# Seven-product input projection in the third and fourth block, and the second layer's modulation as float32 column tiles between the units of output projections

## The reference

```python
def modulation(cond, w, b):
    m = jax.nn.silu(cond) @ w + b          # (2 rows, 1024) @ (1024, 9216)
    return m.reshape(cond.shape[0], 1, N_MOD, D_MODEL)
def modulate_in(x, g_pre, mod, j):
    return rmsnorm(x, g_pre) * (1.0 + mod[:, :, 3 * j + 1]) + mod[:, :, 3 * j]
def gated_residual(x, out, g_post, mod, j, weight):
    return x + weight * mod[:, :, 3 * j + 2] * rmsnorm(out, g_post)
def swiglu(h, w13, w2):                    # w13: 1024 x 5632, w2: 2816 x 1024
    a, g = jnp.split(h @ w13, 2, axis=-1)
    return (jax.nn.silu(g) * a) @ w2
```

## Time and profile before

| what | value |
|---|---|
| runs | 2536.49, 2536.21, 2535.64 us; median 2536.21 us |
| profiled execution, its own time | 2541.83 us |
| its span | 2540.0 us, mean granted clock 0.995 |
| PE busy | 2476.5 us (97%), 15180 matmuls |
| DVE busy | 1581.6 us (62%) |
| ACT busy | 764.9 us (30%) |
| POOL busy | 224.6 us (9%) |
| bytes moved | 278.64 MB, mean 110 GB/s |

### The profile page before, as it was taken

How to read it: one execution, slowest core, us unless ns; L and a number is a source line. 1 busy time by engine, 2 the same in 40 slices (tenths; PEclk the granted TensorE clock), 3 DMA queues, 4 the chain that set the end, 5 groups by cost and what they waited for, 6 DMA issues and landing times. The chain is left out here.

```text
span 2540.0 us, 40285 instructions
## 1 busy us (share of the span) xinstructions
PE 2476.5 (97%) x15180; PEld 2295.7 (90%) x15180; DVE 1581.6 (62%) x2779; ACT 764.9 (30%) x1418; POOL 224.6 (9%) x299
## 2 busy tenths in 40 slices
PE   6999999999998899999999999999999999999998
PEld 5998999799888789989988998899799979989997
DVE  4887588734554678738875885233454458845864
ACT  4111111333444441111124211111331153523432
POOL 0000000201114210000002000000110011201211
PEclk9999999999999999999999999999999999999999
DMA  6554445333223335434551553222312223323332
GB/s 242 160 141 133 133 149 167 107 77 81 48 56 88 88 107 149 134 100 141 149 170 55 150 153 99 80 74 87 96 59 75 87 79 117 83 71 99 88 113 103
DMA packets 385035, 278.64 MB, mean 110 GB/s; under 512 B 39414, under 2 KB 354550, under 8 KB 383894
## 3 DMA queue, kind: packets, MB, share of 16 engines
q1 hardware_dynamic: 384918, 277.06, 36.4%
HBM read 270.04 MB, written 6.94 MB: 109 GB/s over the span
## 5 line engine op out<-in xcount | busy, mean ns | idle before, releaser
L1879 DVE TENSOR_TENSOR w_lo<-w_raw,w_hi 128x1024 fp32r<-128x1024 f32 (+1 forms) x363 | 354.5, 979 | 501.2 <-ACT w_hi L1303 496.8
L1303 ACT ACTIVATE w_hi<-w_raw 128x1024 fp32r<-128x1024 f32 (+1 forms) x363 | 309.2, 854 | 832.4 <-PE psum L921 425.3
L921 PE MATMUL psum<-hT_hi,w_hi 128*128 128x320 f32 x2432 | 554.8, 309 | 4.0 <-DVE w_lo L1879 3.3
L921 PE MATMUL psum<-hT_lo,w_hi 128*128 128x320 f32 x2432 | 554.1, 309 | 0.0
L921 PE MATMUL psum<-hT_hi,w_lo 128*128 128x320 f32 x2432 | 553.8, 309 | 0.0
L921 PEld LDWEIGHTS psum<-hT_hi,w_hi 128*128 128x128 f32 x2432 | 406.3, 188 | 5.7 <-DVE w_lo L1879 2.8
L921 PEld LDWEIGHTS psum<-hT_lo,w_hi 128*128 128x128 f32 x2432 | 406.8, 188 | 0.0
L921 PEld LDWEIGHTS psum<-hT_hi,w_lo 128*128 128x128 f32 x2432 | 406.6, 188 | 0.0
L1848 DVE SCALAR_TENSOR_TENSOR mod_acc<-ada_raw,cond_silu,mod_acc 128x256 f32<-128x256 f32 x896 | 365.4, 479 | 0.0
L848 PE MATMUL psum<-w_hi,act_hi 128*128 128x512 f32 x800 | 318.1, 398 | 4.6 <-DVE w_lo L1879 4.5
L849 PE MATMUL psum<-w_lo,act_hi 128*128 128x512 f32 x800 | 316.3, 395 | 0.0
(11 more groups left out here) (281 smaller groups left out, 3548.1 us busy)
## 6 DMA issues: line engine op xcount, KB each, us to landing
w_raw<-in_ffn_w_dram SPq DMA_DIRECT2D x156, 512.0 KB, 4.1
ada_raw<-in_ada_w_dram SPq DMA_DIRECT2D x128, 512.0 KB, 3.6
w_raw<-in_ffn_w_dram SPq DMA_DIRECT2D x148, 256.0 KB, 2.7
w_raw<-in_ab_w_in_dram SPq DMA_DIRECT2D x28, 512.0 KB, 4.1
w_raw<-in_sc_w_in_dram SPq DMA_DIRECT2D x24, 512.0 KB, 4.0
w_raw_next<-in_ffn_w_dram SPq DMA_DIRECT2D x20, 512.0 KB, 5.2
ada_first<-in_ada_w_dram SPq DMA_DIRECT2D x4, 2048.0 KB, 19.0
held_raw<-in_ffn_w_dram SPq DMA_DIRECT2D x28, 256.0 KB, 3.7
```

The lines of the kernel that those rows point to most:

```text
L921: last = mm(IN[p][0:width, h, 0:HT], a, b[:, k, h * HT:(h + 1) * HT], start=(k == 0 and a is hi and b is hT_hi), stop=(k == KD - 1 and a i ...
L1303: A(dst, src, ACT.Copy).then_inc(w_hi_ok, 1)
L1879: V.tensor_tensor(d_, a, b.bitcast(F32), ALU.subtract).then_inc(w_lo_ok, 1)
```

## The change

Three things are changed together.

1. `PLAIN` names s = 2 and s = 3 as well: 38 more pairs in seven-product form. These blocks also keep x in DRAM and load it again, and load gate, post-norm weights and the next block's column modulation (`load_gate`, `load_cols`) behind the last product of half 1, ahead of the third output unit's weights.
2. The jobs of s = 2 and s = 3 go. The nine modulations of layer 2 (`MODS`: three and one in s = 2, three and one in s = 3, one in s = 5) are made by TensorE in 8 steps each, 72 in all. A step is a float32 matmul on four column tiles: weights `csil[:, :, k]` (128x2), moving `ada_tile` (four times 256 columns), all four tiles into the first 256 columns of one PSUM bank. Steps stand behind output units (`STEP_AT`): in half 0 with three modulations 24 steps behind 17 of the units 1 to 17, with one modulation 8 steps behind 5 units, in half 1 one step behind each of the units 2 to 9. The tiles are 512 KB, in a ring of three, loaded by SP (`load_mods`); the first load of a phase stands behind the fifth output unit's weights (the fifth in half 0, the fourth in half 1) and behind four bias transfers. DVE adds the bias (`modulation_rows`, four operations a modulation) and SP stores the four pieces.
3. Banks, buffer slots and semaphore counts are generalised for these blocks (`out_bank`, `banks`, `RAW_SLOT`); the first output unit of such a half now waits for the last cross sum of the products.

```diff
@@ tables @@
-PLAIN = {5: (3, 0)}
+PLAIN = {2: (3, 0), 3: (3, 0), 5: (3, 0)}
...
-JOBS = {0: (0, 2 * D, (HF, HF), (3, 3)), 2: (1, 0, (HF, HF), (1, 1)), 3: (1, 6 * D, (HF, 0), (1, 0))}
+JOBS = {0: (0, 2 * D, (HF, HF), (3, 3))}
+MODS = {2: ([(1, 0), (1, D), (1, 2 * D)], [(1, 3 * D)]), 3: ([(1, 4 * D), (1, 5 * D), (1, 6 * D)], [(1, 7 * D)]), 5: ([(1, 8 * D)], [])}
+MW = 256
+STEP_AT = lambda half, n: [1 + j * 17 // 24 for j in range(8 * n)] if not half else [2 + j for j in range(8 * n)]
@@ SP: loads of the modulation tiles, called from load_out behind unit u's weights @@
+            def load_mods(ph, u):
+                n = len(ph["mods"])
+                at_u = STEP_AT(ph["half"], n)
+                for j in range(8 * n):
+                    if max(2, at_u[j] + 3 - 2 * ph["half"]) != u:
+                        continue
+                    g = 8 * ph["mb"] + j
+                    if j == 0:
+                        load_bias_rows(ph, 0)
+                        sp.wait_ge(prod_lo_ok, SEVEN * ph["g1"])
+                    if j >= 3:
+                        sp.wait_ge(mod_mm, MM(g - 3))
...
+                    dma(ada_tile[ph["half"]][slot][:], src).then_inc(ada_landed[slot], 16)
@@ PE: the steps, called behind every output unit @@
+            def modulation(ph, u):
+                n = len(ph["mods"])
+                bank = 0 if ph["half"] else 1
+                for j, at_u in enumerate(STEP_AT(ph["half"], n)):
+                    if at_u != u:
+                        continue
+                    g, k = 8 * ph["mb"] + j, j % 8
+                    if j == 0:
+                        pe.wait_ge(q_summed, U_CROSS(ph["g1"] - 1))
+                    elif k == 0:
+                        pe.wait_ge(mrow_ok, MROW(ph["mb"] + j // 8 - 1))
+                    slot, count = TILE(g)
+                    pe.wait_ge(ada_landed[slot], count)
+                    for i in range(4):
+                        last = mm(PS[32 * i:32 * i + 2, bank, 0:MW], csil[:, :, k], ada_tile[ph["half"]][slot][:, i, :], start=(k == 0), stop=(k == 7))
+                    last.then_inc(mod_mm, 1)
@@ PE: bank_free @@
-                            if t == 2:
+                            if t == NT - 1:
                                 pe.wait_ge(q_gated, G_ONE(ph["g1"] - 1))
-                                pe.wait_ge(q_summed, U_TWO(ph["g1"] - 1))
-                            if t == NT - 1:
-                                pe.wait_ge(q_summed, U_CROSS(ph["g1"] - 1))
...
+                        if seven(ph):
+                            if t == 0:
+                                pe.wait_ge(q_summed, U_CROSS(ph["g1"] - 1))
+                            if t >= 2:
+                                pe.wait_ge(out_evac, ph["oe"] + t - 1)
@@ DVE @@
+            def modulation_rows(ph, z):
+                b = ph["mb"] + z
+                dve.wait_ge(mod_mm, MM(8 * b + 7))
...
+                for i in range(4):
+                    rows = slice(32 * i, 32 * i + 2)
+                    V.tensor_tensor(mod_rows[ph["half"]][rows, :], PS[rows, 0 if ph["half"] else 1, 0:MW], mod_bias[rows, :], ALU.add).then_inc(mrow_ok, 1)
```

More of the change, by code:

```diff
@@ L266, in build @@
         assert tail + 8192 + 4096 + HT * 4 <= end, end - tail
+        mod_bias = at("mod_bias", [P, MW], end // 32 * 32 - MW * 4)
+        assert held_at + 3 * 4096 <= end // 32 * 32 - MW * 4
+        mod_rows = [at("mod_rows0", [P, MW], end // 32 * 32 - 2 * MW * 4), at("mod_rows1", [P, MW], held_at - MW * 4)]
+        assert tail + 8192 + 4096 + HT * 4 <= end // 32 * 32 - 2 * MW * 4
+        ada_tile = [[at(f"ada_tile{h}{z}", [P, 4, MW], (tail if h == 0 else j0) + z * 4 * MW * 4) for z in range(3)] for h in range(2)]
+        assert 3 * 4 * MW * 4 <= 8192 + 4096 and j0 + 3 * 4 * MW * 4 <= held_at - MW * 4
         more_hi = at("w_hi_more", [P, 3, KH, P], where["gate"], F32R)
@@ L638, in load_in, with late_rows @@
                         load_job(ph, -1, i)
+            def late_rows(ph):
+                n = len(ph["mods"])
+                last = len(out_units(ph)) - 1
+                for z in range(n):
+                    if STEP_AT(ph["half"], n)[8 * z + 7] + 7 > last:
+                        store_mod_rows(ph, z)
+                        assert z == n - 1
             def load_pairs(s, w, ph, c0):
@@ L860, in turn_x @@
                             pe.wait_ge(mrow_ok, plan[s - 1][-1]["bt"] + 1)
+                    if t == 1 and plan[s - 1][-1].get("mods"):
+                        pe.wait_ge(mrow_ok, MROW(plan[s - 1][-1]["mods_end"] - 1))
                     if t in (1, 4):
@@ L940, in pair_products @@
                         pe.wait_ge(out_evac, ph["oe"] - NT + (1 if q else 0))
+                    elif new == 0 and q == 2 and ph["mb"]:
+                        pe.wait_ge(mrow_ok, MROW(ph["mb"] - 1))
                     elif new == 1 and q == 0:
@@ L1027, in out_phase @@
                             bank_free(d, t)
-                        last = weights(d, k, OUT[d][t], t, k == 0, k == K - 1)
+                        last = weights(d, k, out_bank(ph, d, t), t, k == 0, k == K - 1)
                         if k == K - 1 and t < NT - 1:
@@ L1031, in out_phase @@
                     last.then_inc(pe_unit, 1)
+                    if seven(ph):
+                        modulation(ph, u)
                 if not held:
@@ L1050, in out_phase @@
                             turn_x(s + 1, t - 2)
-                        last = weights(1, k, OUT[1][t], t, z == 0, z == K - 1)
+                        last = weights(1, k, out_bank(ph, 1, t), t, z == 0, z == K - 1)
                         if t == NT - 1 and k in ring:
@@ L2021, in boundary @@
                 split_h(s, NT - 1)
+            def modulation_rows(ph, z):
+                b = ph["mb"] + z
+                dve.wait_ge(mod_mm, MM(8 * b + 7))
+                dve.wait_ge(bias_in, BIAS(b))
+                dve.wait_ge(mod_stored, STORED(b - 1))
+                for i in range(4):
+                    rows = slice(32 * i, 32 * i + 2)
+                    V.tensor_tensor(mod_rows[ph["half"]][rows, :], PS[rows, 0 if ph["half"] else 1, 0:MW], mod_bias[rows, :], ALU.add).then_inc(mrow_ok, 1)
             def out_phase(s, ph):
@@ L2034, in out_phase @@
                             split_held(s, ph, i)
+                    if seven(ph):
+                        for z in range(len(ph["mods"])):
+                            if min(STEP_AT(ph["half"], len(ph["mods"]))[8 * z + 7] + 4, len(units) - 1) == u:
+                                modulation_rows(ph, z)
                     z, r = divmod(u - 1 - LATE[ph["half"]] if late else u, 3)
-                    sooner = 2 if late and not final else 0
+                    sooner = 2 if (late or seven(ph)) and not final else 0
                     if sooner and u == K + 1:
```

104 lines of the change are left out of this document (75 added, 29 removed).

## The result

| | before | with the change |
|---|---|---|
| median of five runs | 2536.28 us | 2548.31 us |
| lowest to highest | 2535.64 to 2537.79 | 2546.09 to 2551.79 |
| profiled execution, its span | 2541.83 us, 2540.0 us | 2547.93 us, 2546.1 us |
| PE busy | 2476.5 us | 2467.1 us |
| matmul records | 15180 | 15288 |

The ratio is 1.0043, 95% interval 1.003 to 1.0055: slower by 12 us. The forecast was "the same" at 2539.2 us, range 2523 to 2557, with 0.38 for slower. The range holds the time, but by the 0.2% that I had set for no change the kernel is slower, and none of the rivals is the reason in the form in which I wrote it: of the one on column tiles and the clock (0.08) the clock did fall, but behind waits and for 9 us, where its price of 93 us was for tiles one after another.

A forecast was written before the change was run, and what follows sets the result against it. PE, busy 97% of the span, was taken as the bound. -58.75 (products) + 31.0 (steps) + 19.3 (visits) + 10.2 (first tiles) + 1.2 = +2.95 us on 2536.21 gave 2539.2 us, range 2523 to 2557.

The forecast's parts named there:

- the one on column tiles and the clock: Slower rival, output phases: column tiles of one bank run serially, or the clock falls; +93 us, 2632 us, chance 0.08.
- The products: Third and fourth blocks: seven-product input phases save 63.35 us; after later waits and sums of jobs, -58.75 us net.
- The steps: Output phases: 72 added modulation steps on PE at 0.43 us each, +31.0 us.
- The visit: Output phases: 55 changes from full width to column tiles and back, 0.35 us each, +19.3 us; lower end 4.4.
- The row of the attention: Profile row with half-width matmuls between full ones, source of the 0.35 us taken for each visit.
- The rival of cheap visits: Faster rival, output phases: a visit costs 0.08 us instead of 0.35; -14.9 us, 2524.3 us, chance 0.14.
- The first tiles: Half 0 of three blocks: PE waits for the first two tiles, 3.4 us a block, +10.2 us.
- late transfers: Slower rival, half 1: tiles land late behind consecutive units, 3 to 13 us each half; +16 us, 2555.2 us, chance 0.24.
- The term of 1.2 us for weights behind the column transfers: Half 1: gate, g_post, column transfers and g_pre precede the third unit's weights; 0.6 us in each of two blocks.

The follow-up runs named there:

- the kernel with one step a modulation: The change with 63 of the 72 modulation steps left out, nine steps in nine visits remaining: 2485.76 us against 2539.12 before.
- the full-width step: Kernel with two early tiles, each step one full-width float32 matmul with identity weights instead of four column tiles: 2518.02 us against 2538.84 before.
- the two edits that shortened the wait in different ways: The change with half 0's first two tiles loaded early, 2531.35 us; the change with half 0's steps one unit later, 2531.64; before 2539.12.
- the first version with two steps a visit: Kernel with two early tiles, two steps at every visit, 36 visits, half 0's last behind the 21st unit: 2551.28 us against 2539.12 before.
- three steps a visit: Up to three steps a visit, 27 visits, with the loads as for two steps and three early tiles: 2527.0 us against 2538.84 before.
- the next two: Two steps a visit with three early tiles, half 0's last behind the 19th unit, 2528.25 us; up to three steps, 2527.0; before 2538.84.

## Why the prediction was right or wrong

**Right by its own steps.** The products: 58.75 us net forecast, 60 by the kernel with one step a modulation; input windows within 1 us of those of the sixth block, but for 1.5 us of low clock in the fourth. The steps: 31.0 us, measured 72 x 0.43 = 31.1 before rounding. 

**The visit, a size.** 55 x 0.35 = 19.3, measured 55 x 0.306 = 16.8. The row of the attention held two widths of tiles and other weights, and was 0.04 too dear. The rival of cheap visits is out; the full-width step shows a visit that costs nothing.

**The first tiles: the step that failed.** I wrote "3.4 us in all, in three blocks, +10.2". The wait was 3.7, 3.5 and 4.3 us. The tiles were issued half a microsecond sooner than reckoned, since a bias transfer took 0.3 us of SP and not 0.45, but the first tile took 5.0, 4.1 and 5.5 us to land and the second 5.9, 5.3 and 6.4, where I had taken 3.6. That is the small part. The large part is the step behind it, which the text had not: behind each of these waits the clock was at 0.50, and some 6 us of PE's work ran at half speed, another 3 us each time, 9.1 in all. I had the row for it, 0.50 behind a stretch in which PE mostly idled, and asked only whether a visit of 1.3 us would do this. The wait that I had reckoned myself, three lines above, was never put to that question. With the measured size of every term the sum is -60 + 31.1 + 16.8 + 11.5 + 9.1 = +8.5 us, against +12.0 in the first comparison and +9.7 on another chip. The 1 to 3 us that are left are within the noise. In the two profiled executions themselves they are found: these differ by 11.0 us from the third block on, and the one with the change has two more falls of the clock, at the first units of the fourth and the sixth block, of some 1.5 us each, which gives 11.5. Not every execution has those two.

That the range held is in part luck: it was made wide for late transfers, which didn't come, and took in a cost of the clock for which it had no term. Three slips of arithmetic stand in the text and moved little: 456 matmuls x 0.147 are 67.0 and not 67.2; 2.8 and 0.4 are 3.2 a block and not 3.4, 0.6 less in all; and the late transfers lose 3 to 10 us a half by their own figures, not 3 to 13.

**Half 1.** The term of 1.2 us for weights behind the column transfers was 0.5: the third unit of each of the two phases waits 0.26 us for its split weights. The rival of late transfers, 0.24, is out: 330 GB/s were moved and no step waited. It took the highest rate that I had seen for the highest there is.

**Whether clock or wait weighs more** is settled by the two edits that shortened the wait in different ways: each gave back more than the whole 11.5 us of waits (15 to 20 us, by the chips compared), though 2.5 to 4.6 us of waits were left. That a long wait is the cause of the fall was shown by taking it away, and by the first version with two steps a visit, where a wait of 5 us at another instruction had the same end. At the tiles, waits of up to 2.2 us had no fall and those of 3.5 in all did; none lies between. That is no limit for other places: with three steps a visit, a wait of 2.3 us at the end of the third block was followed by a fall, and one of 2.3 at the end of the fourth was not. At the ends and beginnings of blocks, where PE turns and waits in short pieces, some executions show a fall and others of the same kernel don't, and what decides there stays open.

## What to carry to other kernels

A wait of PE is priced with what follows it: look at the granted clock behind it, and where it is 0.50, add what the matmuls lose there, here 2.4 to 3.1 us behind waits of 3.5 to 4.7, so that a wait can cost nearly twice its length. When work is moved onto PE, its first operand is what to look at, for a ring that is full later is empty at the start. And small operations in another tiling mode are gathered, as far as their operands and the other engines allow: 0.31 us a visit, for one, two or three steps alike, but the first version here lost all of that to waits, and the next two a part.

## What was not expected of the hardware

- Going from full width to four column tiles and back costs 0.31 us, the same at 52 of 55 visits, while a float32 matmul in full width among split ones costs nothing beyond its own 0.43 us.
- Four column tiles of one bank run side by side, at 0.43 us for 4 x 256 columns in two passes, as those of four banks did in the prologue. By the Trainium skill, PSUM — Partial Sum Buffer, PSUM bank collisions raise a hardware error, different column tiles may access one bank at once; the trace agrees.
- Fully asked, the DMA engines moved 330 GB/s over 32 us, at a busy share of 0.93, beside matmuls at full clock.
